# Rotary rotations taken from TensorE to VectorE shuffles with signed sine tables, and the copies that place the sparse attention's keys moved from ScalarE to VectorE

## The reference

```
# phase A: 16 query heads, 4 key heads of width 64; queries and keys are normalised, then rotated
q = apply_axial_rope(rms_norm(q, q_g), cos, sin)
k = apply_axial_rope(rms_norm(k, k_g), cos, sin)
#   in each half of 32 channels: (x1, x2) -> (x1*cos - x2*sin, x2*cos + x1*sin), x1 and x2 of 16 channels each

# phases N and C: 8 query heads, 2 key groups of width 64; the first 16 channels of each head are rotated
q_rope = _partial_rope(nq, positions)
ks = _partial_rope(p["n_ks"], positions)
kw = _partial_rope(p["n_kw"], positions)
#   r1 = u1*cos - u2*sin ; r2 = u2*cos + u1*sin ; the other 48 channels pass unchanged
```

## Time and profile before

| | |
|---|---|
| median of 3 runs | 1608.32 us (1608.13 to 1611.36) |
| the profiled execution | 1609.1 us; span of its trace 1607.3 us |
| TensorE, VectorE, ScalarE, GpSimd busy | 1533.4, 759.3, 639.4, 684.8 us |
| mean granted clock of TensorE | 0.983 of full |

### The profile page before, as it was taken

How to read it: one execution, slowest core, us unless ns; L and a number is a source line. 1 busy time by engine, 2 the same in 40 slices (tenths; PEclk the granted TensorE clock), 3 DMA queues, 4 the chain that set the end, 5 groups by cost and what they waited for, 6 DMA issues and landing times.

```text
span 1607.3 us, 25456 instructions
## 1 busy us (share of the span) xinstructions
PE 1533.4 (95%) x10002; PEld 1226.4 (76%) x10002; DVE 759.3 (47%) x1767; ACT 639.4 (40%) x1345; POOL 684.8 (43%) x661
## 2 busy tenths in 40 slices
PE   5899999999899899999999899999999989999997
PEld 3777777677688788787877687878788867776887
DVE  4435555455543434534355454733433564455154
ACT  4234444445432533333334353434332344444331
POOL 2534344343432533443435444535255434444462
PEclk8999999999999999999999899999999999999999
DMA  9121111111023322322221322222121221111222
GB/s 395 39 77 42 39 54 53 53 53 54 27 80 105 105 73 79 110 82 80 85 100 53 105 86 79 80 70 88 53 101 57 79 105 53 53 53 53 79 83 75
DMA packets 23143, 128.23 MB, mean 80 GB/s; under 512 B 2417, under 2 KB 4593, under 8 KB 9073
## 3 DMA queue, kind: packets, MB, share of 16 engines
q1 hardware_dynamic: 22880, 126.35, 22.3%
q10 hardware_dynamic: 144, 0.26, 0.0%
HBM read 124.50 MB, written 2.10 MB: 79 GB/s over the span
## 4 chain that ended last, share of the span: by engine, by line
PE 82%; DVE 8%; ACT 3%; issue 3%; POOL 3%; DMA 1%; SPq 0%; POOLq 0%; DVEq 0%; ACTq 0%
PE PS L1516 16%; PE PS L1518 15%; PE PS L1517 15%; PE PS L1596 7%; PE PS L1631 6%; PE PS L1606 6%; PE PS L1509 3%; PE PS L1510 3%; PE PS L1511 3%; DVE sm L2209 2%; PE PS L1684 1%; PE PS L1676 1%; POOL WL L2536 1%; DMA XC<-in_xt 1%; PE PS L1529 1%
## 5 line engine op out<-in xcount | busy, mean ns | idle before, releaser
L2536 POOL TENSOR_TENSOR WL<-W,WH 128x512 fp32r<-128x512 f32 x304 | 400.4, 1332 | 326.7 <-ACT WH L1787 326.5
L1516 PE MATMUL PS<-HX,WH 128*128 128x512 f32 (+1 forms) x1008 | 412.8, 410 | 7.9 <-POOL WL L2536 3.7
L1518 PE MATMUL PS<-HX,WL 128*128 128x512 f32 (+1 forms) x1008 | 391.3, 388 | 0.0
L1517 PE MATMUL PS<-LX,WH 128*128 128x512 f32 (+1 forms) x1008 | 390.7, 388 | 0.0
L1516 PEld LDWEIGHTS PS<-HX,WH 128*128 128x128 f32 x1008 | 193.1, 192 | 54.5 <-issue 14.0
L1518 PEld LDWEIGHTS PS<-HX,WL 128*128 128x128 f32 x1008 | 191.7, 190 | 39.8
L1517 PEld LDWEIGHTS PS<-LX,WH 128*128 128x128 f32 x1008 | 192.7, 191 | 33.3 <-issue 2.6
L1787 ACT CAST WH<-W 128x512 fp32r<-128x512 f32 x320 | 186.9, 619 | 40.9 <-PE PS L1511 21.1
L1873 ACT ACTIVATE AR<-PS,sm 128x768 f32<-128x768 f32 (+4 forms) x160 | 115.5, 722 | 164.1 <-DVE sm L2214 93.7
L2209 DVE TENSOR_REDUCE sm<-PS 128x1 f32<-128x512 f32 (+4 forms) x224 | 150.0, 670 | 51.7 <-PE PS L1596 47.1
L2603 POOL TENSOR_SCALAR AR<-AR,sm 128x768 f32<-128x768 f32 (+1 forms) x96 | 74.8, 779 | 186.9 <-DVE sm L2225 186.9
(11 more groups left out here) (286 smaller groups left out, 2542.7 us busy)
## 6 DMA issues: line engine op xcount, KB each, us to landing
W<-in_wu SPq DMA_DIRECT2D x98, 1024.0 KB, 4.9
AR<-in_wu SPq DMA_DIRECT2D x8, 1024.0 KB, 10.8
AR<-in_biasb SPq DMA_DIRECT2D x32, 256.0 KB, 2.6
XX<-in_xt SPq DMA_DIRECT2D x2, 1024.0 KB, 6.0
XC<-in_xt SPq DMA_DIRECT2D x1, 1024.0 KB, 14.4
out<-XX SPq DMA_DIRECT2D x2, 512.0 KB, 4.1
out<-XX SPq DMA_DIRECT2D x4, 256.0 KB, 2.2
C<-in_cc SPq DMA_DIRECT2D x1, 770.5 KB, 8.4
```

The source lines that it names most:

```text
L1516: e.matmul(o, wh, xh, start=(k == 0), stop=False)
L1517: e.matmul(o, wh, xl, start=False, stop=False)
L1518: t = e.matmul(o, wl, xh, start=False, stop=(k == 7))
L2536: e.tensor_tensor(WL[:, d, a:z], W[:, n % 2, a:z], WH[:, d, a:z].bitcast(F32), ALU.subtract).then_inc(*s_wl_pool.by(n, q))
```

## The change

Every rotation by a matrix product becomes a `stream_shuffle` on VectorE, which permutes partitions inside each group of 32. The signs that the matrix had go into the sine table (for phase A in the constants, for phases N and C by negating the frequencies of the first eight channels). Phase A's `a_query_turn` is split: `a_query_turn` is now the shuffle, and the multiplication by the sines is a task of its own, `a_query_sin`, hooked in after k = 5; `a_query_rope` moves from k = 6 to k = 7. The matrices `p1`, `p2` and an unused `blk` leave the constants, which shrink from 1541 to 1157 columns. `n_key` moves from ScalarE to VectorE.

```diff
+TURN_A = [(i + 16) % 32 for i in range(32)]
+TURN_C = [i + 8 if i < 8 else i - 8 if i < 16 else i for i in range(32)]
...
         for b in range(4, 8):
-            last[b] = [(s_ksin, ((b - 4) // 2,))]
+            last[b] = [(s_kn, ((b - 4) // 2,))]
...
-        def query_turn(pair, pr):
-            aqps[pair, "rot"] = bank(pr.take(("aqr", pair), (s_qsin, (pair,))))
+        def query_turn(pair):
             do("a_query_turn", pair)
+
+        def query_sin(pair):
+            do("a_query_sin", pair)
...
-                yield from gate_group(pair, 0, FX, {2: lambda: query_sums(pair, FC), 3: lambda: query_turn(pair, FC), 6: lambda: query_rope(pair)})
+                yield from gate_group(pair, 0, FX, {2: lambda: query_sums(pair, FC), 3: lambda: query_turn(pair), 5: lambda: query_sin(pair), 7: lambda: query_rope(pair)})
...
# tensor
-            def a_key_rope(m):
-                w.wait_ge(*s_kn(m))
-                e.matmul(K4[m][:, 0:T], c("p1"), krr[m][:, 0:T], start=True, stop=True).then_inc(*s_krot.by(m))
...
-            def a_query_turn(pair):
-                free(w, ("aqr", pair))
-                w.wait_ge(*s_qraw(pair, 1))
-                e.matmul(aqps[pair, "rot"], c("p1"), qT[pair % 2][:, 0:T], start=True, stop=True).then_inc(*s_qrot.by(pair))
...
-            def n_rotate(key):
-                src, (ev, k), dst, o, prev = rot[key]
-                free(w, ("nrot", key))
-                w.wait_ge(*ev(*k))
-                e.matmul(o, c("p2"), src, start=True, stop=True).then_inc(*s_nrot.by(key))
...
# vector
             def a_key_rope(m):
+                w.wait_ge(*s_kn(m))
+                w.wait_ge(*s_ksum())
+                e.stream_shuffle(ksq[m][:, 0:T], krr[m][:, 0:T], TURN_A).then_inc(*s_krot.by(m))
                 w.wait_ge(*s_krot(m))
                 w.wait_ge(*s_cs())
-                e.tensor_tensor(ksq[m][:, 0:T], K4[m][:, 0:T], S1, ALU.mult).then_inc(*s_ksin.by(m))
+                e.tensor_tensor(ksq[m][:, 0:T], ksq[m][:, 0:T], S1, ALU.mult).then_inc(*s_ksin.by(m))
...
             def a_query_turn(pair):
+                w.wait_ge(*s_qsum(pair))
+                w.wait_ge(*s_qraw(pair, 0))
+                e.stream_shuffle(qtmp[pair][:, 0:T], qT[pair % 2][:, 0:T], TURN_A).then_inc(*s_qrot.by(pair))
+
+            def a_query_sin(pair):
                 w.wait_ge(*s_qrot(pair))
-                e.tensor_tensor(qtmp[pair][:, 0:T], aqps[pair, "rot"], S1, ALU.mult).then_inc(*s_qsin.by(pair))
+                w.wait_ge(*s_cs())
+                e.tensor_tensor(qtmp[pair][:, 0:T], qtmp[pair][:, 0:T], S1, ALU.mult).then_inc(*s_qsin.by(pair))
...
             def n_rotate(key):
-                src, by, dst, o, prev = rot[key]
-                w.wait_ge(*s_nrot(key))
+                src, (ev, k), dst, prev = rot[key]
+                w.wait_ge(*ev(*k))
                 w.wait_ge(*s_cv("mk", 3, 1))
-                w.wait_ge(*s_sin())
                 if prev:
                     w.wait_ge(*s_nrope(prev))
-                e.tensor_tensor(tA, o, S2, ALU.mult).then_inc(*s_nsin.by(key))
+                e.stream_shuffle(tA, src, TURN_C).then_inc(*s_nrot.by(key))
+                w.wait_ge(*s_nrot(key))
+                w.wait_ge(*s_sin())
+                e.tensor_tensor(tA, tA, S2, ALU.mult).then_inc(*s_nsin.by(key))
...
+            def n_key(s):        # was in scalar, with e.copy
+                w.wait_ge(*s_nrope(("k", s)))
+                w.wait_ge(*s_vsum(3))
+                kdst = (ksd, kwd)[s]
+                for g in range(2):
+                    for po in (0, 64):
+                        t = e.tensor_copy(kdst[po:po + 64, g, :], kxr[s][64 * g:64 * g + 64, :])
+                t.then_inc(*s_nkd.by(s))
```

More of the change, by code:

```diff
@@ L42 @@
 _n = 0
-for _name, _w in (("id", 128), ("ones", 128), ("tri", 128), ("p1", 128), ("p2", 128), ("blk", 128),
+for _name, _w in (("id", 128), ("ones", 128), ("tri", 128),
                   ("ind", 2), ("inv", 1), ("pick", 2), ("sel", 512), ("cm", 128), ("cmz", 128)):
@@ L119 @@
     tensor_tensor = tensor_scalar = scalar_tensor_tensor = tensor_copy = nothing
-    tensor_reduce = reciprocal = memset = affine_select = tensor_tensor_scan = dma_start = nothing
+    tensor_reduce = reciprocal = memset = affine_select = tensor_tensor_scan = dma_start = stream_shuffle = nothing
 class Waits:
@@ L869, in build @@
         values((4,))
-        query_turn(0, vr)
+        query_turn(0)
+        query_sin(0)
         values((5,))
@@ L1274, in rotate @@
         def rotate(key, src, by, dst):
-            rot[key] = (src, by, dst, bank(ONE.take(("nrot", key), (s_nsin, (key,)))), rotlast[0])
+            rot[key] = (src, by, dst, rotlast[0])
             rotlast[0] = key
@@ L2005, in n_hidden @@
                     e.activation(hid[m][:, 0:62], w1[m][1][:, 0:62], ACT.Gelu_apprx_tanh).then_inc(*s_hid.by(m))
-            def n_key(s):
-                w.wait_ge(*s_nrope(("k", s)))
-                w.wait_ge(*s_vsum(3))
-                kdst = (ksd, kwd)[s]
-                for g in range(2):
-                    for po in (0, 64):
-                        t = e.copy(kdst[po:po + 64, g, :], kxr[s][64 * g:64 * g + 64, :])
-                t.then_inc(*s_nkd.by(s))
             def cmp(tile):
@@ L2046, in scalar @@
                                m_num_sq=m_num_sq, m_den=m_den, n_query=n_query, n_cmp_in=n_cmp_in, n_key_raw=n_key_raw, n_hidden=n_hidden,
-                               n_key=n_key, cmp=cmp, n_gate=n_gate, cmp_turn=cmp_turn, x_ga=x_ga, x_gb=x_gb))
+                               cmp=cmp, n_gate=n_gate, cmp_turn=cmp_turn, x_ga=x_ga, x_gb=x_gb))
         def vector(e, w):
@@ L2524, in vector @@
                                m_gate=m_gate, m_qk=m_qk, m_den=m_den, m_var=m_var, m_scale=m_scale, n_rotate=n_rotate, n_blocks=n_blocks,
-                               n_cmp_out=n_cmp_out, n_value=n_value, cmp=cmp, n_gate=n_gate, x_merge_a=x_merge_a, x_wb=x_wb, final=final))
+                               n_cmp_out=n_cmp_out, n_key=n_key, n_value=n_value, cmp=cmp, n_gate=n_gate, x_merge_a=x_merge_a, x_wb=x_wb, final=final))
         def gpsimd(e, w):
@@ L2738, in constants @@
     put("tri", np.where(k <= q, 0, NEG).astype(f))
-    p1 = np.zeros((P, P), f)
-    p2 = np.zeros((P, P), f)
-    for h in (0, 64):
-        for a in (0, 32):
-            for i in range(16):
-                p1[h + a + 16 + i, h + a + i] = -1
-                p1[h + a + i, h + a + 16 + i] = 1
-        for i in range(8):
-            p2[h + 8 + i, h + i] = -1
-            p2[h + i, h + 8 + i] = 1
-    put("p1", p1)
-    put("p2", p2)
-    blk = np.kron(np.eye(2), np.ones((64, 64))).astype(f)
-    put("blk", blk)
-    put("ind", blk[:, ::64])
+    put("ind", np.kron(np.eye(2), np.ones((64, 1))).astype(f))
     inv2 = np.power(f(500000.0), -np.arange(8, dtype=f) * f(2.0 / 16)).astype(f)
@@ L2756, in constants @@
     for h in (0, 64):
-        iv[h:h + 8, 0] = inv2
+        iv[h:h + 8, 0] = -inv2
         iv[h + 8:h + 16, 0] = inv2
@@ L2777, in constants @@
     put("pick", pick)
-    return o, np.concatenate([np.cos(full), np.sin(full)], 1).astype(f)
+    sign = np.where(np.arange(P) % 32 < 16, -1, 1).astype(f)[:, None]
+    return o, np.concatenate([np.cos(full), sign * np.sin(full)], 1).astype(f)
 def lay_out(a):
```

6 lines of the change are left out of this document (3 added, 3 removed).

## The result

The changed kernel takes 1612.28 us (median of 18 runs, 1607.4 to 1615.2); the kernel before took 1608.43 us in 18 runs beside it. The ratio is 1.0023, 95% interval 1.0014 to 1.0032: **slower by 2.3 to 5.1 us**, where 8.3 faster was forecast. The profiled execution took 1612.1 us, its span is 1610.4 us.

The account below looks back on a forecast made before the run. TensorE, busy for 95% of the span, was taken as the bound; -0.5 - 2.1 + 0.4 - 1.7 + 0 - 5.1 = -9.0 us against 1609.1 gave 1600.1, stated as 1600, range 1593.5 to 1605.5 us.

Parts of the forecast that it names:

- So TensorE waits 0.86 longer: Pairs 1 to 4: the post's chain is anchored at GpSimd, so four rotations' 3.4 us are given back; +0.4 us net.
- Pairs 5 and 6: Phase A: the post waits for TensorE's product, not the addition, so both rotations count; -1.7 us.
- the rotations of phase N: Phase N: the ending chain stays on TensorE through all six removed rotations; -5.4 us if VectorE keeps up.
- The shuffle's price: VectorE: a shuffle of 512 elements costs 0.69 us, like the multiplication by the sines; allowed up to 2.2 us.
- Pair 7, "I take 0": Pair 7's scores: TensorE's 0.86 us go into the wait for addition and cosines; 0, bounds -0.9 and +0.5 us.
- The keys: Keys and pair 0: TensorE gains 2.6 us, less a 0.5 us wait for a value tile's copy; net -2.1 us.
- behind them lie 3.1 us more; the shorter queue of TensorE moves both ends together: Phase N, `kcd`: VectorE's 1.7 us of copies fit into its 2.19 us wait; +0.3 us for bank waits, bounds 0 and +3.
- (d) Slower: TensorE's clock: Rival: new waits in pairs 1 to 4 bring half-clock stretches, losing 12 us; about 1611 to 1615 us, chance 0.06.
- The ring of banks: Keys: value tile 5 takes another bank, 0.5 us wait; phase N: +0.3 us for bank waits behind later evacuations.
- The constants, -0.5: Start of the kernel: 0.197 MB less to load at 395 GB/s; -0.5 us, bounds 0 and 0.5.

Follow-up runs that it names:

- phase N's part alone: The kernel before with only phase N's six shuffles and the placing copies on VectorE: -1.5 us at full clock, 3.5 us more lost to the clock.
- phase A's: The changed kernel with phases N and C as before, phase A as changed: -1.3 us at full clock, 1.6 us more lost to the clock.

## Why the prediction was wrong

- **"So TensorE waits 0.86 longer", pairs 1 to 4**: right in mechanism and size. Forecast 1.1 us and in pair 1 2.1, measured 1.05 and 2.28. The stage came out at +1.2 for +0.4 because TensorE waits 1.14 for 0.41 us in pair 4 for a small VectorE operation of another part (L2050, which takes 0.79 us beside GpSimd and took 0.18), which was not looked for.
- **Pairs 5 and 6**, **the rotations of phase N**: right, -1.8 for -1.7 and -5.0 for -5.4.
- **The shuffle's price**: nearly right, 0.74 us for 0.69, and with it a 0.01 us load of its pattern. The Trainium skill, "VectorE: DVE Perf Modes", section "The perf-mode tier table", gave an estimate of 0.6 by the share of elements; the trace has 0.74, and the measurement decides.
- **Pair 7, "I take 0"**: mis-sized, +0.65. The sines were priced as the ones that lose by contention. In phase A they kept their price (0.67 us on average), and it is GpSimd's cosines that lose. The shuffle's end releases both at once:

```profile
410.00 0.67 DVE L2167 TENSOR_TENSOR AR<-AR,CS 128x512 f32<-128x512 f32 x1
...
410.00 1.80 POOL L2597 TENSOR_TENSOR AR<-AR,CS 128x512 f32<-128x512 f32 x1 [0.16 <-DVE AR L2162]
```

  0.52 us more than the 1.28 of the earlier trace rows, and 0.23 from the later start: the scores wait 1.79 us. The rule of the Trainium skill on the shared pair ("SBUF — State Buffer", "Who interferes with whom") puts the loss on whichever starts second; here both start at 410.00, and the trace shows the loss on GpSimd's side, not on the sines' as the prediction had it. By forms:

```profile
L2597 POOL TENSOR_TENSOR AR<-AR,CS 128x512 f32<-128x512 f32 x8 | 11.3, 1408 | 0.2 <-DVE AR L2162 0.2
```

  The keys lost by the same: 1.78 us for each, a wait of 0.91 for a value tile's copy, -1.5 for -2.1.
- **Phase N, "behind them lie 3.1 us more; the shorter queue of TensorE moves both ends together": the step that failed.** The two ends did not move together. VectorE's chain does not hang on TensorE but, through GpSimd's queue, on a load that came only 1.4 us earlier, and it was longer than priced: the second four copies 2.69 us for 1.7, both additions 1.7 us for the 0.69 of before. `kcd` was done at 1282.67, 0.7 us earlier than before, where TensorE was 5.6 us earlier; the slack of 3.1 us was eaten and a wait of 1.92 left, where none was forecast. Ahead of it stood 0.5 us for weights. With what the clock lost behind it the stage cost +7.3 us for +0.3.
- **"(d) Slower: TensorE's clock"** was priced as two rare stretches of 15 us, from 12 us of loss on, and its sign was to be sought in phase A. What came was 6.2 us on average, 3.5 with phase N's part alone and 1.6 with phase A's. With a gain of 2.8 us in place of 9 it needs no 12 us to end slower: the rival was judged against the full gain. Its time, 1611 to 1615, is the one that came, with other parts than it was made of.
- **The ring of banks** was looked at for phase N and the keys only. Near the end it costs 2 us (1.1 and 0.8 us of waits), a term that the sum does not have.
- **The constants, -0.5**: not seen. ScalarE's wait for the input is 0.47 for 0.91 us, but the start scatters between -1.0 and +0.4 us over the traces.

## What to carry to other kernels

Work taken from the bounding engine makes it early everywhere behind, so ask of each operand it will meet what *that* hangs on: a chain that hangs on a load or on another engine's queue does not come earlier, and the gain ends in its slack. Where a saved step also took a buffer of a ring, follow the ring to the end of the program. And split every run into its length at full clock and the clock's loss: here they moved against each other. Look in the trace whether TensorE was busy in the half-clock stretches: where it stood idle they cost nothing.

## What the runs showed of the hardware

Two useless matmuls (1.94 us) in a gap of TensorE made the kernel 3 us faster at the same length at full clock (1577.6 for 1577.4 us): the gain is the clock's. When a VectorE operation with two inputs in memory and a GpSimd operation start at the same time, it was GpSimd that became longer, 1.28 to 1.80 us, about by three quarters of the other's 0.67; when GpSimd had started 0.14 us earlier, VectorE's addition took 1.7 us for 0.69. VectorE's copies from memory to memory become longer too: four of 64 x 512 took 1.73 us, and 2.69 beside GpSimd's low parts.
